# Product blocks of the first MLP matmul: a sixth weight buffer, another order of loads and sums, and one of four weight sums moved to GpSimd

## The reference

```python
h = rmsnorm(x, g_pre_mlp[i]) * (1.0 + scale_f) + shift_f
y = squared_relu_mlp(h, w_mlp_in[i], w_mlp_out[i])     # square(relu(h @ w_mlp_in)) @ w_mlp_out
x = x + gate_f * rmsnorm(y, g_post_mlp[i])
```

## Time and profile before

| | |
|---|---|
| median of 3 runs | 2344.43 us (2339.22 to 2344.59) |
| the profiled execution | 2344.84 us, its span 2343.0 us |
| instructions | 31846 |
| granted TensorE clock, mean over the span | 0.96 |
| busy: PE, PEld, DVE, ACT, POOL | 2174.4, 1873.3, 1772.4, 968.8, 348.4 us |
| the seven-product blocks | 961.9 to about 1716.8 us |

### The profile page before, as it was taken

How to read it: one execution, slowest core, us unless ns; L and a number is a source line. 1 busy time by engine, 2 the same in 40 slices (tenths; PEclk the granted TensorE clock), 3 DMA queues, 4 the chain that set the end, 5 groups by cost and what they waited for, 6 DMA issues and landing times.

```text
span 2343.0 us, 31846 instructions
## 1 busy us (share of the span) xinstructions
PE 2174.4 (93%) x11815; PEld 1873.3 (80%) x11815; DVE 1772.4 (76%) x1931; ACT 968.8 (41%) x1222; POOL 348.4 (15%) x202
## 2 busy tenths in 40 slices
PE   6999999999999997988878888887899999999998
PEld 4688888778878886888878888887888888888886
DVE  7977666777876366866667676667789898988998
ACT  4453433333442253444434444444454444444353
POOL 1000000000000013000000000000006364545443
PEclk9999999999999999988888889888899999999999
DMA  9957665745544442455555455554456745665854
GB/s 363 356 187 235 216 198 160 244 143 167 160 146 144 162 145 102 137 185 179 183 171 171 163 166 174 172 171 149 144 180 216 240 163 190 239 228 183 284 195 183
DMA packets 316125, 444.73 MB, mean 190 GB/s; under 512 B 19341, under 2 KB 183505, under 8 KB 310361
## 3 DMA queue, kind: packets, MB, share of 16 engines
q1 hardware_dynamic: 315746, 442.87, 56.1%
q10 hardware_dynamic: 248, 0.08, 0.0%
HBM read 383.10 MB, written 59.79 MB: 189 GB/s over the span
## 4 chain that ended last, share of the span: by engine, by line
PE 73%; DMA 9%; DVE 9%; issue 4%; ACT 2%; POOL 1%; DVEq 1%; SPq 0%; POOLq 0%; ACTq 0%
PE pair L975 23%; PE pair L977 22%; PE pair L976 22%; DMA sw_raw<-in_w_mlp_in 9%; DVE sw_lo L2798 3%; DVE sw_raw L2776 1%; ACT sw_hi L1928 1%; PE pair L1198 1%; DVE sw_raw L2769 1%; PE pair L1082 1%; PE pair L1056 1%; DVEq L2707 1%; DVE hid_f L2708 0%; DVE pair L2809 0%; PE pair L1073 0%
## 5 line engine op out<-in xcount | busy, mean ns | idle before, releaser
L975 PE MATMUL pair<-in_hi,sw_hi 128*128 128x256 f32 x896 | 283.8, 317 | 126.2 <-DVE pair L2809 126.0
L1928 ACT ACTIVATE sw_hi<-sw_raw 128x1024 fp32r<-128x1024 f32 x196 | 207.4, 1058 | 371.3 <-PE pair L977 207.9
L975 PE MATMUL pair<-in_hi,w_hi 128*128 128x512 f32 (+1 forms) x832 | 341.6, 411 | 12.5 <-DVE w_lo L2114 9.4
L975 PE MATMUL pair<-v_op,hid_r 128*128 128x512 f32 x896 | 348.9, 389 | 1.0 <-issue 0.9
L977 PE MATMUL pair<-v_op,hid_r 128*128 128x512 f32 x896 | 348.6, 389 | 0.0
L976 PE MATMUL pair<-v_op,hid_r 128*128 128x512 f32 x896 | 348.6, 389 | 0.0
L2893 DVE TENSOR_TENSOR v_op<-v_raw,v_op 128x1024 fp32r<-128x1024 f32 x192 | 295.5, 1561 | 55.3 <-ACT v_op L2061 54.3
L977 PE MATMUL pair<-in_hi,w_lo 128*128 128x512 f32 (+1 forms) x832 | 323.3, 389 | 0.0
L976 PE MATMUL pair<-in_lo,w_hi 128*128 128x512 f32 (+1 forms) x832 | 322.1, 387 | 0.0
L2061 ACT ACTIVATE v_op<-v_raw 128x1024 fp32r<-128x1024 f32 x192 | 203.2, 1061 | 274.3 <-PE pair L977 268.0
L3159 POOL TENSOR_TENSOR v_sum<-v_raw,v_raw 128x512 f32<-128x512 f32 x60 | 149.2, 2514 | 1089.2 <-DVE v_raw L2908 1089.2
(11 more groups left out here) (324 smaller groups left out, 4127.1 us busy)
## 6 DMA issues: line engine op xcount, KB each, us to landing
v_raw<-in_w_mlp_out SPq DMA_DIRECT2D x128, 512.0 KB, 5.3
sw_raw<-in_w_mlp_in SPq DMA_DIRECT2D x112, 512.0 KB, 4.5
hid_r<-hid_scratch SPq DMA_DIRECT2D x112, 512.0 KB, 6.3
hid_scratch<-hid_r SPq DMA_DIRECT2D x28, 1792.0 KB, 9.4
am_item<-in_w_ada SPq DMA_DIRECT2D x64, 512.0 KB, 8.4
af_item<-in_w_ada SPq DMA_DIRECT2D x64, 512.0 KB, 4.8
w_raw<-in_w_in SPq DMA_DIRECT2D x96, 256.0 KB, 3.5
w_raw<-in_w_in SPq DMA_DIRECT2D x160, 128.0 KB, 3.3
```

Source lines behind the costliest of these rows:

```text
L975: pe.matmul(dst, a[0], b[0], start=start, stop=False, skip_group_check=onto)
L1928: act.activation(sw_hi[n % 3][:, :, :], sw_tile(u, SW_OPERAND[i])[:, :, :], ACT.Copy).then_inc(sw_hi_done, 1)
```

## The change

1. A sixth raw buffer, where `gf_item[0]` lay; SUM always lies in buffer 3, A22 in buffer 2 (even blocks) or 5 (odd).
2. SP's order: A11 and A22 together after the low part of P7; then a gate load; then A21 after `sum_4`; up to two gate loads of the next block; both stores of hidden rows, one after the other; A12 last.
3. `sum_1` of all 28 blocks is issued by GpSimd; VectorE no longer has it after the low part of P4.
4. The gate's items have 512 columns in place of 1024, so there are 64 in place of 32, in blocks 1 to 24 (three, three and two in turn). The third of a block is used after the low part of P4. The four quarters of the gate are finished at blocks 7, 13, 19 and 25 in place of 13, 15, 25 and 26.
5. At the end, one wait of ScalarE's second operand of the next stage is for the low part of P5 of the last block in place of that of P4.

```diff
-        SW_RAW_AT = (0, 4, 8, 12, 32)
-        sw_raw = [at(f"sw_raw{n}", [P, XQ, P], R_C + KIB * SW_RAW_AT[n]) for n in range(5)]
+        SW_RAW_AT = (0, 4, 8, 12, 32, 36)
+        sw_raw = [at(f"sw_raw{n}", [P, XQ, P], R_C + KIB * SW_RAW_AT[n]) for n in range(6)]
-        gf_item = [at(f"gf_item{n}", [P, 1024], (R_C + 36 * KIB, R_B + 28 * KIB)[n]) for n in range(2)]
+        gf_item = [at(f"gf_item{n}", [P, 512], R_B + (28 + 2 * n) * KIB) for n in range(2)]
...
-        SW_SLOT = ((0, 1, 2, 3, 4), (1, 0, 3, 2, 4))
+        SW_SLOT = ((0, 1, 2, 3, 4), (1, 0, 5, 3, 4))
...
-        for g in range(2 * GF_ITEMS):
-            GF_AT[1 + 3 * (g // 4) + (0, 1, 1, 2)[g % 4]].append(g)
-        GF_PART = {13: 0, 15: 1, 25: 2, 26: 3}
+        for g in range(4 * GF_ITEMS):
+            GF_AT[1 + 3 * g // 8].append(g)
+        GF_PART = {7: 0, 13: 1, 19: 2, 25: 3}
...
                 sp.wait_ge(sw_lo_done, step_end(u, F_P7))
                 if following:
                     load_quarter(u + 1, A11)
+                    load_quarter(u + 1, A22)
                 else:
                     sp.wait_ge(sw_used, step_end(u, F_P7))
                     load_m2(0, B11)
                     load_m2(0, B22)
+                for g in GF_AT[u][2:]:
+                    load_gf(g)
+                if following:
+                    if u - 1 in GF_PART and GF_PART[u - 1] < 3:
+                        load_g_post(GF_PART[u - 1] + 1)
+                    sp.wait_ge(sw_sum, SW_SUM_0 + sums_of(u, S_4))
+                    load_quarter(u + 1, A21)
+                    for g in GF_AT[u + 1][:2]:
+                        load_gf(g)
                 if stored:
                     store_hidden(b - 1, 0)
-                if following:
-                    sp.wait_ge(sw_lo_done, step_end(u, F_P6))
-                    sp.wait_ge(sw_sum, SW_SUM_0 + sums_of(u, S_4))
-                    load_quarter(u + 1, A21)
-                if stored:
                     store_hidden(b - 1, 1)
                 if following:
-                    sp.wait_ge(sw_lo_done, step_end(u, F_P5))
-                    load_quarter(u + 1, A22)
-                    for g in GF_AT[u + 1]:
-                        load_gf(g)
-                    if u - 1 in GF_PART and GF_PART[u - 1] < 3:
-                        load_g_post(GF_PART[u - 1] + 1)
                     sp.wait_ge(sw_lo_done, step_end(u, F_P3))
                     load_quarter(u + 1, A12)
...
@@ VectorE, strassen_in(u) @@
                 if u == 0:
-                    sum_1(0)
                     sum_3(0)
...
-                for g in GF_AT[u][1:]:
+                for g in GF_AT[u][1:2]:
                     gf_step(g)
...
                 split_lo_step(n0 + F_P4)
-                if u + 1 < SUBS:
-                    sum_1(u + 1)
+                for g in GF_AT[u][2:]:
+                    gf_step(g)
...
@@ GpSimd, after its sums ahead of the blocks @@
+            def sum_1(u):
+                for role in (A21, A22):
+                    done, count = sw_arrived(u, role)
+                    pool.wait_ge(done, count)
+                if u:
+                    pool.wait_ge(sw_lo_done, step_end(u - 1, F_P4))
+                pool.tensor_tensor(sw_tile(u, SUM)[:, :, :], sw_tile(u, A21)[:, :, :], sw_tile(u, A22)[:, :, :], ALU.add)\
+                    .then_inc(sw_sum, 1)
+
+            for u in range(SUBS):
+                sum_1(u)
```

More of the change, by code:

```diff
@@ L601, in build_block @@
         gf_row, GF_ROW_0 = rows_in, 16 * 9
-        sw_in, SW_IN_0 = x_in + [c_in], 16
+        sw_in, SW_IN_0 = {0: x_in[0], 1: x_in[1], 2: x_in[2], 4: x_in[3], 5: c_in}, 16
         gf_in, GF_IN_0 = [bfg_in, cum_out], 16
@@ L695, in load_gf @@
             def load_gf(g):
-                half, k = divmod(g, GF_ITEMS)
+                part, k = divmod(g, GF_ITEMS)
                 if g > 1:
                     sp.wait_ge(gf_used, g - 1)
-                src = w_ada_t[:, k:k + 1, GATE_F + 1024 * half:GATE_F + 1024 * half + 1024].rearrange("p o n -> p (o n)")
+                src = w_ada_t[:, k:k + 1, GATE_F + 512 * part:GATE_F + 512 * part + 512].rearrange("p o n -> p (o n)")
                 sp.dma_start(gf_item[g % 2][:, :], src).then_inc(gf_in[g % 2], 16)
@@ L897, in _ @@
             sp.wait_ge(sw_lo_done, ALL_STEPS)
-            sp.wait_ge(gf_used, 2 * GF_ITEMS)
+            sp.wait_ge(gf_used, 4 * GF_ITEMS)
             load_m2(0, B12)
@@ L1940, in gf_high @@
             def gf_high(part):
-                act.wait_ge(gf_used, GF_ITEMS * (part // 2 + 1))
+                act.wait_ge(gf_used, GF_ITEMS * (part + 1))
                 if part:
@@ L2057, in split_operand @@
                 elif i == 1:
-                    act.wait_ge(sw_lo_done, ALL_STEPS - 1)
+                    act.wait_ge(sw_lo_done, step_end(SUBS - 1, F_P5))
                 else:
@@ L2761, in _ @@
             x_low(1)
[L2763 to L2770, removed]
             def sum_3(u):
@@ L2817, in gf_step @@
                     dve.wait_ge(gf_used, g)
-                part = gg[:, 1024 * half:1024 * half + 1024]
-                dve.scalar_tensor_tensor(part, gf_item[g % 2][:, :], c_act[:, k:k + 1], part, ALU.mult, ALU.add)\
+                columns = gg[:, 512 * part:512 * part + 512]
+                dve.scalar_tensor_tensor(columns, gf_item[g % 2][:, :], c_act[:, k:k + 1], columns, ALU.mult, ALU.add)\
                     .then_inc(gf_used, 1)
```

## The result

The changed kernel takes 2219.85 us (median), a ratio of 0.9472 to the kernel before (95% interval 0.9453 to 0.949): 5.3% faster, as forecast (2216, range 2158 to 2262). Of its four executions one took 4063.22 us at a lower clock; it is in the median and not in the ratio, and the other three took 2218.42 to 2220.98. Its profiled execution took 2218.42 us, with a span of 2216.2.

What follows compares the result with a forecast made beforehand. A buffer and a queue order, delaying A22, set TensorE's wait. 13 pairs x 43.2 + 13 (stores) + 6 (clock) = 581 us against 706.75: 126 less, 2 at the end, 1 in the first block; 2344.8 - 129 = 2216, range 2158 to 2262.

Steps and rivals of the forecast that it cites:

- A pair: Even plus odd block of the stage: 43.2 us against 54.4, with P3 waiting 2.07 us in even blocks, 0.8 in odd.
- The turn: GpSimd and VectorE alternate by whole instructions, so sum_1 costs VectorE 2.30 us where it has work, in place of 1.14.
- the 25 us that I gave for the sum on VectorE: Keeping sum_1 on VectorE with the rest changed: some 25 us saved if VectorE never stood waiting for A21.
- The stores: Two hidden stores back to back delay ScalarE's relu in 8 even blocks, 1.6 us each: 13 us; A12 costs no more.
- The clock: In the stage, half of 8 longer waits bring the low clock: 4 falls x 1.5 us = 6 us.
- The border that I drew: Wait length deciding clock falls: stage waits from 2.95 us up brought the low clock, 3.06 us at 906.34 did not.
- my signs of being wrong: Sums above 4 us, A21 over 6 us to land, granted clock still 0.88, or a step other than P3 waiting.
- B: TensorE becomes the bound of the stage, 20.3 us a block remain: 2162 us; chance 0.13.
- C: The low clock stays in the stage: 2230 us with one fall a pair, 2256 with one every block; chance 0.22.
- D: A sum on GpSimd takes 6.7 us and holds VectorE for all of it: 2368 us; chance 0.06.
- E: A21 meets traffic as A22 did, lands after 9.8 us, and P3 waits as now: 2340 us; chance 0.05.
- F: Stores take 9.4 us one after the other, delaying P2's low part: 101 us instead of 13, 2318 us; chance 0.06.

Runs made afterwards that it cites:

- Number 8: Kernel before with the sixth buffer, half-width gate items and A22 loaded right after A11; old store order, sum_1 on VectorE: 2218.99 us (0.9479).
- Number 4: Changed kernel with A22 loaded late again, after the low part of P5, behind A21 and the gate loads: 2281.01 us (0.974).
- number 12: Kernel before with only sum_1 moved to GpSimd: 2318.38 us (0.9891).
- number 10: number 9 with sum_1 on VectorE, make_c22 ahead of sum_3 and, in odd blocks, P7's low part ahead of the first hidden low part: 2169.56 us (0.9251).
- number 11: number 10 with sum_1 on GpSimd: 2180.82 us (0.9299).
- number 1: Changed kernel with sum_1 back on VectorE, right after the third gate item and ahead of combine: 2215.68 us (0.9451).
- number 5: Changed kernel with both stores ahead of the second gate load and sum_1 on VectorE: 2202.99 us (0.9402).
- number 3: Changed kernel with both stores issued ahead of the second gate load: 2206.81 us (0.9415).
- number 9: number 3 with store 0 issued at the start of an odd block: 2205.22 us (0.9405).
- 6: Changed kernel with make_c22 issued ahead of sum_3 instead of behind it: 2213.51 us (0.9451).

## Why the prediction was right

**What bounded the kernel.** A22's load, by its buffer. Number 8 shows it: the buffer and the early load, with the gate items that make room, give the whole gain (0.9479 against 0.9472). Number 4, which undoes the early load alone, takes half of it back. The engine of the sum gives 1.1% while A22 is late (number 12) and nothing or less after that. The gate's smaller items were not tried by themselves.

**A pair.** I had 43.2 us for a pair before stores and clock, 44.7 with them, 581 in all. 582.73 were measured, but this is in part luck, as two errors cancel. My sum has 37.3 us of waits and 13 for the stores, 50 together; TensorE stood idle for 41.4. Even blocks wait 2.59 us on average, the odd ones 0.26, not 0.8. And my sum has 524 us of matmuls (20.16 a block) and 6 for the clock, 530 together; TensorE was busy for 541.3. Less 7.3 for the clock (below) that is 534, or 20.5 a block. The 0.4 beyond 20.16 were in the 27.18 of the kernel before as well. They are, among others, gate rows and matmuls that start after a wait, and I had left them out. 9 us too much and 11 us too little make the 2 us by which 581 is off.

**GpSimd.** 2.30 us for 1024 columns was right for a sum alone: the shortest is 2.39, the median 2.65 with its turn. The turn is as I read it from one pair of rows: 2.74 for an operation of 0.69. It costs VectorE 43 us in all in the changed kernel, an estimate from the means of the lines that are stretched: 14 x (2.16 - 0.69) for line 2707, 14 x (1.32 - 0.69) for 2705, 196 x (1.290 - 1.220) for the low parts. On VectorE the 28 sums would take 28 x 1.14 = 32. That the difference is 11, as between numbers 10 and 11, is chance: number 11 has 30 us of stretching, all in even blocks, and there a block pays 2.2 us in place of 1.14. The weak step was the 25 us that I gave for the sum on VectorE if it never stood waiting for A21: number 1 against the change and number 5 against number 3 gave 4 each, and in numbers 1 and 5 it does stand for A21, for 12.6 and 15.0 us.

**The stores.** I had 13 us: eight even blocks, those behind an odd block with three gate items, 1.6 us each. The eight are right. Against number 9, where no relu waits, the wait for `make_c22` is 0.7 to 1.2 us longer in just these blocks, 1.02 on average, and 0.03 in the other five. That is 8.2 us, and with TensorE's other waits, 3.9 us, which number 9 doesn't have either, 12. So the term fits better than its working. Number 3 measured 13, with the relu's wait falling by 23 us. The second of two stores took 11.1 to 13.9 us to land where I had 12.8. The 8.5 us of the earlier trace rows were not a lone store's, as I had read them: the load of A11 was issued 0.4 us before it, and in the changed kernel the first of two stores took 6.8 to 10.3. I had also said that A12 behind the stores costs no more; ScalarE waits 8.2 us for it.

The Trainium skill (DMA: Bandwidth & Descriptors, Anatomy of one DMA) gives its fit for DMAs that GpSimd issues; these are SP's. By the fit both stores would have landed after 10.4 us, an estimate. The trace does not agree with it: the second store took 11.1 us at least, from its own issue.

**The clock.** I counted 4 falls that cost 1.5 us each. There are 5 in these 26 blocks, each 3.4 us long, with TensorE busy for 16.7 us of the 17.1. At the lower level a matmul starts 0.21 us after the last one, at the higher one 0.12:

```profile
1028.57 0.41 PE L974 MATMUL pair<-in_hi,sw_hi 128*128 128x256 f32 x1
1028.78 0.41 PE L975 MATMUL pair<-in_lo,sw_hi 128*128 128x256 f32 x1
...
1031.86 0.28 PE L975 MATMUL pair<-in_lo,sw_hi 128*128 128x256 f32 x1
1031.98 0.28 PE L976 MATMUL pair<-in_hi,sw_lo 128*128 128x256 f32 x1
```

So a fall costs 3.4 x (1 - 0.120/0.213) = 1.5 us, and the five 7.3 in place of 6. By the same working the 100 us that TensorE was busy less at the lower level (116.7 to 16.7) are worth 44 us, the whole fall of its busy time.

But the falls don't follow the length of the wait, by which I had chosen them. They come with waits of 3.21, 2.16, 2.55, 3.19 and 2.16 us (ending at 1026.95, 1071.13, 1117.41, 1297.52 and 1341.71; the third begins 0.4 us before the wait's end, the others 0.4 to 1.5 us behind it), and not with 3.20 (1432.79) or 2.90 (1162.64). Windows about 2 us after the end of two waits of 3.2 us:

```profile
1029.00:1030.00 1.00, 1.00 (x6) 1.00 (x6) 1.00 (x3) 0.35 (x1) 0.00 (x0) 0.50 0.00 0
1435.00:1436.00 1.00, 1.00 (x11) 1.00 (x10) 1.00 (x3) 0.21 (x2) 0.00 (x0) 1.00 0.00 0
```

The border that I drew, a wait of 3.06 us at 906.34 without a fall, was one execution's answer. The same wait stands ahead of the stage in all 14 profiled executions, 3.06 to 3.08 us long, in code that no edit touches. In 6 the level had fallen when the matmul began, the changed kernel's among them; in 4 it fell 1.1 to 1.3 us later; in 4 it didn't fall. The changed kernel's row, and the window behind it (columns as in rows 2):

```profile
905.94 0.77 PE L974 MATMUL pair<-in_hi,w_hi 128*128 128x512 f32 x1 [3.08 <-ACT w_hi L1488]
...
905.94:908.80 2.86, 2.86 (x7) 2.28 (x8) 0.00 (x0) 2.83 (x4) 2.86 (x1) 0.50 0.56 160
```

That 5 falls are near my 4 is luck, then; what decides a fall stays open.

**Rivals.** One of my signs of being wrong did come: steps other than P3 wait, seven times, 3.9 us in all. It is too little to count against the forecast. B (TensorE the bound) is what number 10 reached, not the change. C is refuted by a clock of 0.99 against 0.88, D by the 2.4 to 3.4 us of the sums. E: A21 landed about 4.5 us after its issue, ahead of the stores. F: the second store took 13.9, not 18.8.

## What to carry to other kernels

When an engine that works in program order stands for a load, ask what lets that load be issued. Here it was a buffer. A sixth buffer, the smaller items that make room for it and one early issue gave all that they gave together with the move of a sum to another engine and a new store order. Then follow the chain to its next late part: the waits came up one after the other (P3 for `make_c22`, the relu for the stores, P2 for A12, P7 behind a hidden low part), and the edits to the changed kernel in numbers 1, 3, 6 and 9 gave 4 to 15 us each, where all of them together gave 50 and left TensorE busy for 99% of the stage (2169.56 us, which beats both kernels). Work handed to an engine that takes turns with the first is not off it: count its whole length, and look at what the first engine is doing at that time: the sum on GpSimd gained 25 us while VectorE would have stood waiting, and cost up to 16 once it wouldn't.

## What was not expected of the hardware

Waits of the same length were answered by the clock in both ways, and waits of 2.16 us were followed by the lower level where one of 3.20 was not. The fall can also come after the wait: at 1026.95 the first matmul still took 0.36 us, and the level fell 1.3 us later. A load that follows two stores in SP's queue took 11.3 us to land (A12 issued at 1226.0), although the second store had been issued 3.1 us earlier and landed at 1234.2; A21, issued at 1218.11 with no store ahead of it, took 4.3. And the time between the last block and the end of the kernel grew by 2.3 us with no edit there but one wait. TensorE has new waits at the seam (1.37 and 0.38 us), of which I have not tried the cause. Numbers 1, 8, 10 and 11 have them too (1.6 and 0.4 us), numbers 3, 6 and 9 don't; it stays open.
